# Running two attention forms piece by piece on one core, with the delta rule's buffers moved into the weight ring

## The reference

```
mod = silu(c) @ w_ada + b_ada                     # shift, scale, gate, twice: 6 x 1024 columns
h   = rmsnorm(x) * (1 + sc1) + sh1
p   = h @ w_in                                    # q1 k1 v1 lr g1 | q k v (short convolution, silu) | a b | z
o1  = rmsnorm(gla_chunked(q1, k1, v1, log_a, state_gla)) * silu(g1)      # 4 heads, 64 x 128 state
o2  = rmsnorm(gdn_chunked(q, k, v, g, beta, state_gdn)) * silu(z)        # 4 heads, 128 x 128 state
x   = x + gt1 * (concat(o1, o2) @ w_out)
x   = x + gt2 * ffn(rmsnorm(x) * (1 + sc2) + sh2)   # layer 0: SwiGLU of 2816; layer 1: top 2 of 8 experts of 3584
```

## Time and profile before

| | |
|---|---|
| Median of 3 runs | 2136.74 us (2135.57 to 2136.97) |
| The profiled execution | 2136.68 us, span 2134.9 us |
| Mean granted TensorE clock | 0.943 |
| Busy | PE 91%, DVE 69%, ACT 51% of the span |
| DMA | 505.30 MB, mean 237 GB/s |
| Input projection, layer 0 | about 40 to 155 us |
| Attention and its output projection, layer 0 | about 155 to 400 us |
| Input projection and attention, layer 1 | about 659 to 979 us |
| Experts | about 1075 to 2134 us |

### The profile page before, as it was taken

One profiled execution on the slowest core, in us unless ns is written; L12 is line 12 of the kernel. 1 busy time (PEld: TensorE's weight loads), 2 busy tenths in 40 slices (PEclk: granted clock), 3 DMA queues, 4 the chain that ended last, 5 costly groups with the idle time before them and its releaser, 6 DMA issues.

```text
span 2134.9 us, 25466 instructions
## 1 busy us (share of the span) xinstructions
PE 1953.1 (91%) x10368; PEld 1600.1 (75%) x10368; DVE 1475.0 (69%) x1827; ACT 1093.5 (51%) x1105; POOL 12.6 (1%) x27
## 2 busy tenths in 40 slices
PE   6998688899998987789699999999999999999995
PEld 3894476799997963767587878778787887878883
DVE  3943656754437734747578878888888887888885
ACT  3741233333226621333367767676676766767663
POOL 0000000000000000000000000000000000000000
PEclk9996798999999987889599999999999999999998
DMA  9343514343353336133188989989898998989990
GB/s 388 120 171 114 234 39 184 119 158 133 107 176 124 139 121 261 75 124 138 60 329 330 352 325 358 334 335 350 323 363 323 344 344 327 358 319 355 336 353 26
DMA packets 70616, 505.30 MB, mean 237 GB/s; under 512 B 8064, under 2 KB 8224, under 8 KB 11872
## 3 DMA queue, kind: packets, MB, share of 16 engines
q1 hardware_dynamic: 68112, 488.29, 61.0%
q0 software_dynamic: 2384, 15.34, 2.0%
HBM read 494.88 MB, written 8.72 MB: 236 GB/s over the span
## 4 chain that ended last, share of the span: by engine, by line
issue 53%; PE 31%; DVE 12%; ACT 2%; DMA 1%; SPq 0%; DVEq 0%; POOL 0%; ACTq 0%; POOLq 0%
PE bank L574 30%; DVE wlo L399 1%; DVE work L1542 1%; ACT work L1134 1%; ACT L1134 1%; DMA raw<-in_ada 1%; DVE work L1763 1%; DVE work L1543 0%; DMA raw<-in_w_in 0%; DVE hT L1462 0%; DVE work L1634 0%; DMA work<-in_s_gla 0%; DVE hl L1470 0%; ACT whi L394 0%; DVE hT L1495 0%
## 5 line engine op out<-in xcount | busy, mean ns | idle before, releaser
L399 DVE TENSOR_TENSOR wlo<-raw,whi 128x2048 fp32r<-128x2048 f32 (+1 forms) x412 | 919.7, 2261 | 211.6 <-ACT whi L394 210.3
L394 ACT ACTIVATE whi<-raw 128x2048 fp32r<-128x2048 f32 (+1 forms) x412 | 761.5, 1889 | 78.0 <-PE bank L574 73.8
L1134 ACT ACTIVATE work<-bank 128x512 f32<-128x512 f32 (+6 forms) x295 | 134.7, 474 | 478.9 <-PE bank L574 395.6
L574 PE MATMUL bank<-whi,hg_high 128*128 128x512 f32 x896 | 369.1, 412 | 1.5 <-DVE hg_low L1910 1.5
L574 PE MATMUL bank<-whi,hg_low 128*128 128x512 f32 x896 | 354.9, 396 | 0.0
L574 PE MATMUL bank<-wlo,hg_high 128*128 128x512 f32 x896 | 354.9, 396 | 0.0
L574 PE MATMUL bank<-hh,whi 128*128 128x320 f32 x944 | 300.2, 318 | 29.1 <-DVE hl L1470 18.6
L574 PE MATMUL bank<-work 128*128 128x128 f32 (+12 forms) x1552 | 261.5, 331 | 37.5 <-ACT work L1134 11.7
L574 PE MATMUL bank<-hh,wlo 128*128 128x320 f32 x944 | 293.3, 311 | 0.0
L574 PE MATMUL bank<-hl,whi 128*128 128x320 f32 x944 | 293.2, 311 | 0.0
L574 PEld LDWEIGHTS bank<-work 128*128 128x128 f32 (+4 forms) x1552 | 196.8, 203 | 87.9 <-issue 33.1
(11 more groups left out here) (238 smaller groups left out, 1632.1 us busy)
## 6 DMA issues: line engine op xcount, KB each, us to landing
raw<-in_moe SPq DMA_DIRECT2D x336, 1024.0 KB, 4.8
raw<-in_ada SPq DMA_DIRECT2D x56, 1024.0 KB, 7.9
raw<-in_w_in SPq DMA_DIRECT2D x30, 1024.0 KB, 4.9
raw<-in_gu SPq DMA_DIRECT2D x22, 1024.0 KB, 4.8
raw<-in_down SPq DMA_DIRECT2D x16, 704.0 KB, 4.0
raw<-in_w_out SPq DMA_DIRECT2D x8, 1024.0 KB, 9.3
work<-in_s_gdn POOLq DMA_DIRECT2D x2, 2048.0 KB, 9.0
out_gdn_s<-work POOLq DMA_DIRECT2D x2, 2048.0 KB, 7.4
```

The source lines that it names most:

```text
L394: ac.activation(whi[:, part(n), 0:width(n)], raw[:, n % SLOTS, 0:width(n)], ACT.Copy).then_inc(S("w_high"), 1)
L399: ve.tensor_tensor(wlo[:, n % SLOTS, 0:width(n)], raw[:, n % SLOTS, 0:width(n)], whi[:, part(n), 0:width(n)], ALU.subtract).then_inc(S("w_ ...
L574: return pe.matmul(out, lhsT, rhs, start=start, stop=stop, **k)
L1134: return ac.activation(out, in_, func, **k)
```

## The change

- **Interleaving.** GLA and GDN no longer follow each other. On each engine one written list runs a piece of the one, then a piece of the other: scores of tile 0, delta tile 0's transpositions, GLA's values, and so on. The sample tile of GLA (its values, spreading, state products and additions) runs beside the levels of the joint inversion (`samples_beside(v)` on PE and DVE).
- **Banks.** The delta rule keeps B0, B4, B2, B3 (`NB`), GLA and the head norms B5, B6, B7 (`XB`). In the inversion, Y and its update share one bank per half tile (`IBANK`). The spread of the root takes 5 matmuls over 3 banks instead of 4 over 4 (`SPREAD_AT`). The output projection's first unit goes to B0 (`OBANK`).
- **Buffers.** `DSET` lies in `whi` (name `wscr`). So the 4 output slots are copied into parts 0 and 1 only (`PART`), one slot ahead instead of two, and the slots after them are copied after the norm.
- **Half the spreading.** `GVM` and the delta rule's equivalent are 64 x 512 instead of 64 x 1024: each half of the rows holds its own 4 sequences (`seq4`), and the state products take 32 rows each instead of 64.
- **Head norms and modulation.** GLA's head norm stands between the ends of delta tiles 0 and 1 (its sum after `keys(0)`, its spread after `keys(1)`). The 24 pieces of the three modulation sets are dealt out anew; the first half of set x+2 stands after the sample tile's inversion.
- **Input projection.** Four banks instead of two (`PBANK`: B0, B1, B2, B7); unit u waits for unit u-4.
- **POOL.** The load of the delta rule's sample states is issued after GLA's last state product.

```diff
-        GVM = v3(take(1024), NSEQ)
+        GVM = v3(take(512), 4)
+        take(256)
...
+        DSET = [[wscr[:, at + 512 * i:at + 512 * (i + 1)] for i in range(9)] for at in (PARTS * HALF - 9 * 512, 0)]
+        DY = DSET[0][7]
+        D01, D34 = w(0, 512), w(2 * TL, 512)
...
+        NB, XB = (B[0], B[4], B[2], B[3]), (B[5], B[6], B[7])
+        IBANK = (NB[0:2], NB[2:4], NB[0:2])
...
+        OBANK = [B[5 + j % 2] if j else B[0] for j in range(KD)]
...
+        SPREAD_AT = [(0, 0, T, 1, 0), (1, 0, T, 2, 0), (2, 0, T, 0, 0), (3, 0, 192, 1, T), (3, 192, T, 2, T)]
...
+        PART, BEFORE = {}, {}
+        turns, latest = 0, {}
+        for n in SPLITS:
+            out = [n - a for a in AT_OUT if a <= n < a + H_OUT]
+            if out:
+                PART[n], turns = out[0] % 2, 2
+            else:
+                PART[n], turns = turns % PARTS, turns + 1
+            BEFORE[n] = latest.get(PART[n])
+            latest[PART[n]] = n
+
...
+                after(po, "gla_ss_mm", l, GH)
+                po.dma_start(DS, A["s_gdn"][l, :, :, :, :]).then_inc(S("gdn_state_in"), 16)
                 after(po, "gdn_state", l, 2)
-                po.dma_start(DS, A["s_gdn"][l, :, :, :, :]).then_inc(S("gdn_state_in"), 16)
...
+                for h, f, t, bank, at in SPREAD_AT:
+                    ins = mm(XB[bank][:, at:at + t - f], ident[:, 32 * h:32 * h + 1].to_broadcast([P, P]), rs[:, f:t])
...
-                    if u >= 2:
-                        after(pe, "proj", l, u - 1)
...
+                    if u >= 4:
+                        after(pe, "proj", l, u - 3)
...
+                        ins = mm3(PBANK[u % 4][:, 0:T], wh[:, k, c], wl[:, k, c], hh[:, k, :], hl[:, k, :], k == 0, k == KD - 1)
...
+                def gla_sample_state(h):
+
+                    lo, p = 64 * (h % 2), h // 2
+                    after(pe, "gla_vm", l, h + 1)
+                    if h == 2:
+                        after(pe, "gla_sstate", l, 1)
+                    for c, bank in enumerate((XB[2], XB[0])):
+                        rows = slice(32 * c, 32 * c + 32)
+                        ins = mm(bank[lo:lo + 64, :], GKDT[rows, p * P + lo:p * P + lo + 64], GVM[rows, :, :])
+                    ins.then_inc(S("gla_ss_mm"), 1)
+
...
-                for first in (0, 2):
-                    group = (0, 1) if first == 0 else (2,)
-                    for i in group:
-                        prepare(i)
-                    invert(group)
-                    for i in group:
-                        finish(i)
-                finish_heads(("heads", 2 * l + 2), w(4 * TL, TL), lambda: ada_turn(x + 2))
...
+                def samples_beside(v):
+
+                    if v in (1, 2):
+                        gla_sample_values(v - 1)
+                    if v > 2:
+                        gla_sample_state(v - 3)
+
+                gla_scores(0)
+                ada(x, 0)
+                turn(0)
+                ada(x, 1)
+                gla_values(0)
+                ada(x, 2)
+                turn_back(0)
+                gla_scores(1)
+                ada(x, 3)
+                products(0)
+                ada(x, 4)
+                turn(1)
+                gla_values(1)
+                ada(x, 5, 6)
+                turn_back(1)
+                gla_scores(2)
+                products(1)
+                ada(x, 7)
+                invert((0, 1), samples_beside)
+                ada_turn(x)
+                keys(0)
+                heads_sum(("heads", 2 * l + 1), QK)
+                new_values(0)
+                ada(x + 1, 0, 1)
+                outputs(0)
+                ada(x + 1, 2)
+                settled(0)
+                keys(1)
+                heads_spread(("heads", 2 * l + 1))
+                new_values(1)
+                ada(x + 1, 3, 4)
+                outputs(1)
+                ada(x + 1, 5)
+                settled(1)
+                turn(2)
+                ada(x + 1, 6, 7)
+                turn_back(2)
+                products(2)
+                ada_turn(x + 1)
+                invert((2,), lambda v: None)
+                ada(x + 2, 0, 1, 2, 3)
+                keys(2)
+                new_values(2)
+                outputs(2)
+                ada(x + 2, 6, 7)
+                after(pe, "do", l, 3)
+                heads_sum(("heads", 2 * l + 2), w(4 * TL, TL))
+                ada_turn(x + 2)
+                heads_spread(("heads", 2 * l + 2))
...
+                        rows = slice(32 * c, 32 * c + 32)
+                        ins = mm(SBANK[h % 2][c][:, :], DSET[0][2][rows, h * P:(h + 1) * P], vm[rows, 0:512])
...
+                gla_tokens(0)
+                exponentials(1)
+                squares_qk(0)
+                gla_result(0)
+                masks(0)
+                turned_back(0)
+                gla_tokens(1)
+                row_decay(0)
+                exponentials(2)
+                squares_qk(1)
+                gla_result(1)
+                masks(1)
+                turned_back(1)
+                gla_tokens(2)
+                row_decay(1)
+                ada_rows(x)
+                invert((0, 1), lambda v: gla_result(2) if v == 2 else None)
+                keys(0)
+                new_values(0)
+                rsqrt_seed(("heads", 2 * l + 1))
+                outputs(0)
+                keys(1)
+                new_values(1)
+                outputs(1)
+                squares_qk(2)
+                masks(2)
+                ada_rows(x + 1)
+                turned_back(2)
+                row_decay(2)
+                invert((2,), lambda v: None)
+                keys(2)
+                high.to(AT_OUT[l] + 1)
+                new_values(2)
+                outputs(2)
+                after(ac, "gla_fin", l, 1)
...
-                        high.to(AT_OUT[l] + j // 2 + LEAD)
+                        high.to(AT_OUT[l] + j // 2 + 2)
...
+                def spread(h):
...
+                        after(ve, "gla_ss_mm", l, h)
+                    do(tt(GVM[0:TS, :, :], mid(GVT[0:TS, h * P:(h + 1) * P], 4), last(cst("seq4", TS), GV), ALU.mult), "gla_vm")
+
+                def decayed(p):
+
+                    after(ve, "gla_o_mm", l, 3)
+                    do(tt(GSS[p], GSS[p], last(v3(gEB_[:, :], 2)[:, p, :], GV), ALU.mult))
+
+                def added(p):
+
+                    after(ve, "gla_ss_mm", l, 2 * p + 2)
+                    for c, bank in enumerate((XB[2], XB[0])):
+                        ins = tt(GSS[p][:, 4 * c:4 * c + 4, :], GSS[p][:, 4 * c:4 * c + 4, :], v3(bank[:, :], 4), ALU.add)
+                        go(ins) if c == 0 else do(ins, "gla_sstate")
...
+                def samples_beside(v):
+
+                    if v == 0:
+                        gla_scored(2)
+                    if 1 < v < 6:
+                        spread(v - 2)
+                    if v in (3, 4):
+                        decayed(v - 3)
+                    if v == 4:
+                        added(0)
+                    if v == 6:
+                        added(1)
+
+                arguments(1)
+                gla_scored(0)
+                normalize(0)
+                gla_carried(0)
+                operands(1)
+                strict(0)
+                arguments(2)
+                gla_scored(1)
+                normalize(1)
+                gla_carried(1)
+                operands(2)
+                strict(1)
+                invert((0, 1), samples_beside)
+                o1, tag1 = hT[:, 0:GH, :], ("heads", 2 * l + 1)
+                after(ve, "gla_o", l, 3)
+                heads_square(tag1, o1, QK)
+                heads_root(tag1)
+                ada_add(x)
+                first_state()
+                heads_gate(o1, G1, col(f"glan{l}"))
+                second_state()
+                heads_scale(tag1, o1, "gla_fin", False)
+                normalize(2)
+                strict(2)
+                ada_add(x + 1)
+                invert((2,), lambda v: None)
+                sample_rows()
                 low.to(AT_OUT[l] + 1)
                 after(ve, "do", l, 3)
 
```

More of the change, by code:

```diff
@@ L188, in build @@
         raw = sb("raw", [P, SLOTS, HALF])
+        with ExitStack() as over:
+            wscr = over.enter_context(nc.sbuf_tensor("wscr", [P, PARTS * HALF], F32))
         whi = sb("whi", [P, PARTS, HALF], F32R)
@@ L739, in _ @@
-                    after(pe, "gla_o", l, i + 1)
-                ada_turn(x)
-                finish_heads(("heads", 2 * l + 1), QK, lambda: ada(x + 1, 0, 1, 2, 3))
-                after(pe, "gla_fin", l, 1)
-                def prepare(i):
-                    (t0, nt), (DVB, DKB, DKD, DM, DMB, DT, DU, DY, DX) = TILES[i], DSET[i % 2]
-                    for b, bank in enumerate((B[0], B[4], B[2])):
-                        if i == 1 and b == 2:
-                            after(pe, "dat", l, 1)
-                            after(pe, "drowe", l, 1)
+                    ins.then_inc(S("gla_o_mm"), 1)
@@ L752, in prepare, with turn @@
```

(47 more changed lines are left out.)

364 lines of the change are left out of this document (159 added, 205 removed).

## The result

The changed kernel takes 2055.64 us (median of 4 runs, 2054.89 to 2057.72) against 2136.47 before: ratio 0.9624, 95% interval 0.9607 to 0.964. It is 80.8 us faster; I had said 66.7. Run again beside the experiments, the same program had a median of 2054.38 (2050.28 to 2057.04), ratio 0.9619 (0.9606 to 0.9632): that is 0.6 us outside the range, so on which side of its edge the time falls is chance.

A forecast was written before the change was run, and what follows sets the result against it. Attention was taken as a chain with no engine full. Per layer 55.6 - 10.1 - 16.5 + 0.3 = 29.3, twice 58.6, with the projection's 8.5 67.1: 2136.7 - 67.1 = 2069.6, said as 2070; range 2055 to 2096, the forecast's own 2058 to 2085.

The forecast's parts named there:

- Part 1: Input projection: four banks cover PE's waits for ACT, saving 4.7 + 3.8 = 8.5 us over both layers; bounds 0 and 9.2.
- Part 2: GLA's first arguments to DVE's first inversion level, prompt tiles interleaved with delta preparation: 103.1 to 47.5 us, saving 55.6 per layer.
- Part 3: Joint inversion hosting GLA's sample tile: grows by 10.1 us per layer, from 39.0 to 49.1; bounds 8 and 22.5.
- Part 4: Last update of the joint inversion to the sample tile's outputs: 49.9 to 66.4 us, losing 16.5 per layer; bounds 62 to 72.
- Output projection, -0.3: Sample tile's outputs to the first feed-forward unit: the 512-wide spreading there saves 0.3 us per layer.
- the third: Attention: overlap tighter than the sum, clock staying up in delta preparation, 62 us behind the inversion; 2053 us, chance 0.08.
- Rival 1: Joint inversion: it hosts nothing for free and grows by 22.5 us instead of 10.1; 2094 us, chance 0.15.
- rival 2: Input projection: gains nothing, because DVE is busy almost without a break and PE meets the next low part; 2078, chance 0.10.
- rival 4: Joint inversion: the clock stays at its lower level through it, 95 us instead of 49; 2161 us, chance 0.03.
- Part 1's sign: Input projection: no wait of PE for ACT over 0.2 us.
- levels 1 and 2 near 9: Joint inversion: levels holding GLA's sample values take near 9 us each, at clock 1.00.
- levels 3 to 5 near 7.9: Joint inversion: these levels, hosting state products, take near 7.9 us each, at clock 1.00.

The follow-up runs named there:

- same-rows run: Changed kernel, but both matmuls of each pair of state products read rows 0 to 31: 2065.93 us, ratio 0.9663 to the kernel before.
- the five: Changed kernel with products ahead of next scores, new values ahead of head-norm sum, set addition before root, last pieces behind second norm's sum, low part sooner: 2019.5 us.
- the six moves: The kernel with the five moves, plus three of four modulation pieces put between the levels of the sample tile's inversion: 2021.9 us, ratio 0.9456 to before.

## Why the prediction was right, and what was mis-sized

- **Direction and mechanism.** Right: a chain of short steps, shortened by running two of them at once. The size was 14 us short, most of it with one sign; that the time still fell inside the range was luck. The sum of the bounds (2056) was passed, since the inversion grew by less than its lower bound of 8.
- **Part 1, 8.5 us.** Mis-sized: 6.0 here, 8.0 in the repeated execution, where the clock holds. DVE's low part was named, but PE waited 2.6 us for it, not 0.6, because the waits for ACT had cost more than they show (6.9 against 5.2 up to unit 16). The clock lost behind that wait was in no term.
- **Part 2, -55.6.** -57.0. The two waits (3.1 and 1.9 said) were 5.3 and 2.7; the 3.8 us I had added for the clock are mostly in them, as 3.0 more. The 51 us for half clock throughout did not come: the mean granted clock was 0.85. The clock falls behind PE's idle time, as these two steps of the changed kernel show:

```profile
165.00:170.00 5.00, 2.17 (x12) 1.41 (x10) 4.57 (x13) 1.79 (x3) 0.00 (x0) 0.74 0.00 0
170.00:175.00 5.00, 5.00 (x54) 2.62 (x53) 0.04 (x1) 0.38 (x1) 0.00 (x0) 0.58 0.12 29
```

- **Part 3, +10.1.** The step that failed, the growth of the inversion by its guests (the work of the sample tile put between its levels): +4.6. It makes 11 of the missing 14 us. The errors are below.
- **Part 4, +16.5.** +14.8, with the PE gap of 4.6 (4.8 said). Half of the 1.7 is the last state product, 1.07 instead of 1.9 (+0.8 in the same-rows run).
- **Output projection, -0.3.** The four products there save 3.4 us per layer (1.13 against 1.98). The second head norm took 3.5 us more, at a clock of 0.56 to 0.75. Two unpriced terms that cancel: the term came out by luck.

The errors of part 3, first in rows of the kernel before that I hadn't shown: two update instructions of DVE one level apart, then the whole group of matmuls that starts with the sample values, and ACT's reading of GLA's sample outputs (from separate views of PE and ACT).

```profile
276.99 0.42 DVE L1762 TENSOR_TENSOR work<-work,bank 128x256 f32<-128x256 f32 x1 [1.37 <-PE bank L574]
...
283.30 0.42 DVE L1762 TENSOR_TENSOR work<-work,bank 128x256 f32<-128x256 f32 x1 [1.37 <-PE bank L574]
```

```profile
183.52 12.29 PE L574 MATMUL bank<-work 128*128 128x64 f32 x44 [2.44 <-DMA work<-in_s_gla]
...
192.24 0.38 ACT L1134 ACTIVATE hT<-bank 128x256 f32<-128x256 f32 x1 [11.38 <-PE bank L574]
```

A level took 6.31 us, so one with sample values grew by 1.28, not 2.7. By level, the 5.5 us between 10.1 and 4.6 are:

- **Levels 1 and 2: 2.6 instead of 5.4.** First, the values were read too long: they end before 192.24, not at 195.8, where that group of matmuls ends with the first state product in it. That is 8.7 us at the half clock, and 2 x 2.30 = 4.6 at full instead of 6.2. Second, a guest hides more than the 0.6 us gap: the level's 48 matmuls and the guest's 20 take 7.59 in all, so 2.30 of guest cost 1.28. Third, a slip: half of 6.2 less the gap is 2.5, and I had put 2.7.
- **Levels 3 to 5: 2.6 instead of 4.65.** Level 3 grew by 0.65, level 4, where DVE sticks out, by 1.98, level 5 by nothing. The same-rows run, with the products at 1.93, prices their duration at 0.7; the other 1.3 is again work that the levels hide.
- **The first level: 0.6 shorter than before.** The clock was 0.65 there before and 1.00 now.

So 0.7 of the 5.5 is tried by an experiment; the other 4.8 are read from the traces and not tried by themselves.

Of the rivals, the third gave the nearest time (2053), but for another reason: the clock did not stay up in part 2, part 4 did not take 62, and most of the gain beyond the forecast was in the inversion. Rival 1 erred to the other side (22.5 against 4.6 measured), rival 2 is refuted by the 6.0 us of the projections, and rival 4 by the clock of 1.00 through the inversion with all guests in it. Part 1's sign held: PE waits for ACT nowhere in the projection. The signs "levels 1 and 2 near 9" (7.59) and "levels 3 to 5 near 7.9" (6.96, 8.29 and, as before, 5.53) missed.

## What to carry to other kernels

Price a matmul that changes its rows by where it stands in the array too: here two independent ones in different row strips shared their time. A long stage that keeps PE full is a good host, for more than its visible gaps and for the clock: the guests ran at the full clock there, and at 0.50 for most of a stage of their own. Removing a short wait of PE can give back more than the wait shows (6.9 us for 5.2 here), and the next late event then costs more than the sum of the waits says. Where one bank serves two sets in turn, look for the reader that frees it and put it into the first idle moment: one moved addition gave 12.7 us.

## What the runs showed of the hardware

- Two fp32 matmuls of 32 rows, rows 0 to 31 and 32 to 63, into different banks: 1.07 us together (64 output partitions) or 1.13 (128). Both in rows 0 to 31: 1.93 or 1.98.
- Equal instruction lists don't have equal clocks. The second head norm of layer 0 took 12.07 or 9.78 us in two executions of the changed program. Where only other stages differ it varies as much: 8.5 or 12.3 us as it stood before, 9.6 to 10.0 or 11.8 to 11.9 with the five and the six moves. Which of the two comes is open; a gain under 3 us per layer can't be read from one profile that crosses it. A stage that keeps PE nearly full repeats: from the first inversion subtraction to the head norm, 44.96 to 44.98 us in 18 of 18 (nine profiles with these guests, two layers).
- The same holds behind the PE wait for DVE's low part in the projection: 112.74 us for the stage in four profiles with waits of 2.57 to 2.60 us (one of them the code of before with four banks), 111.23 in five others, two with 2.62 and three with 2.15 to 2.26.
- Gaps of PE between matmuls cost more than they show: seven waits of 5.2 us in all, once gone, brought PE 6.9 us forward, and 2.30 us of independent matmuls in a level with a gap of 0.56 lengthened it by 1.28.
